# The sums of the down projection's weights in a DeepNorm decoder layer: made by transfers in DRAM from slab 6 on, in place of GpSimd beside the feed-forward slabs

## The chip, the cores and the metric

The kernel runs on one core of a Trainium2 chip. The metric is the device time of one execution, in microseconds (us), lower is better. The core has a matrix engine (PE, TensorE), a vector engine (DVE), a scalar engine (ACT), GpSimd (POOL) and an engine that only issues transfers (SP); all of them have queues of their own and meet through semaphores. 16 DMA engines carry the transfers of all queues.

## What is computed

One post-norm decoder layer on x of 512 tokens by 1024 channels, all in float32. The attention half comes first, then the channel mixer, whose last product is the one that the change is about:

```
proj   = x @ w_in                     # q,k,v of two attentions, forget logits, two gates
o_f    = forgetting_attention(...)    # 8 heads of 64
o_s    = sliding_window_sink_attention(...)
merged = sigmoid(g_f) * (o_f @ w_o_fox) + sigmoid(g_s) * (o_s @ w_o_swa)
h      = layer_norm(alpha * x + merged @ w_out)
ff     = (silu(h @ w_gate) * (h @ w_up)) @ w_down      # w_down: 2816 x 1024
out    = layer_norm(alpha * h + ff)
```

## The kernel before

Every float32 product is made of three matmuls: each operand is split into a high part, a float32r copy that ACT makes (`sh`, `xh`, `ah`), and a low part, the difference that DVE makes (`sl`, `xl`, `al`); PE adds high times high, low times high and high times low (L1375 to L1377, L1688 to L1690).

Weights come as **slabs** of 128 x 1024 elements, 512 KB each: 0 to 5 the queries, keys and values of the sliding window, 6 to 17 those of the forgetting attention, 18 to 33 the gates, 34 to 41 the output projections of the two branches, 42 to 49 w_out, 50 to 93 the gate and up matrices of the feed-forward. SP loads slab n into one of two buffers `raw` (L438) as soon as the low part of slab n - 2 has been made. ACT makes the high part of slab n (L574, L805 in the feed-forward) while PE works on slab n - 3, and DVE the low part behind it (L847, L855). ACT and DVE are in-order engines, and their programs are written out step by step: in step n ACT evicts the result of slab n - 1, takes the transposed probabilities and the exponentials of the attention units of that step, and then calls `slab_hi(n + 3)`. A unit is one head's attention: scores before a slab, its softmax on DVE and ACT, its transposes after the second of the slab's eight column blocks, and its product with the values two slabs later. Units 0 to 7 (sliding window) have their scores in steps 6 to 13, units 8 to 15 (forgetting attention) in steps 19 to 26. In steps 16 to 18 there are no units at all.

The **down projection** is made by a scheme of seven products instead of eight. For a pair of 128-row blocks of w_down (11 pairs) and its two column halves there are four quarters W11, W12, W22, W21, each 128 x 512. Besides them the scheme needs the sums

```
T1 = W11 + W12      T3 = W12 + W22      T2 = T1 + W22      T4 = T2 + W21
```

of all 11 pairs. They lie in an internal DRAM tensor `tw` of 11 x 4 x 128 x 512 floats (11.5 MB), and SP and ACT wait for all of them (semaphore `t_stored`) before the first of the 77 items of the down projection, which SP loads at L460, from `tw` or from the weights.

Before the change POOL makes the sums in the feed-forward stage: `weight_sums(i)` waits for the 1 MB load of pair i (`stage`, L523), makes the sums with three additions (L530, L533, L535), stores them (`tw`, L537) and issues the next load. Between two pairs POOL makes three sums of hidden activations (`hidden_sums`, L546 to L549), which need the results of the feed-forward slabs. Ahead of all that POOL's program holds four rotary multiplications (L500; the last one belongs to slab 5), the loads of the residual and of the first layer norm's parameters once all 16 attention units are done (`pv_done`, L503 to L505), and three halves of layer norm rows (L512). DVE reads `res` from that load for the first time at L1094.

Of the kernel before, what the change touches and what calls it, by code (L numbers as in the profile page):

```python
# [24 lines left out]
ALU = mybir.AluOpType  # L25
# [6 lines left out]
P = 128  # L32
# [18 lines left out]
N_QF = 6  # L51
# [18 lines left out]
PAIRS = FT // 2  # L70
# [3 lines left out]
W11, W12, W22, W21 = range(4)  # L74
T1, T3, T2, T4 = range(4)
# [97 lines left out]
def program(nc, xT, x, slabs, vk_slabs, wdn, rope, rope_tok, sel, b_forget, sinks, ln1_g, ln1_b, ln2_g, ln2_b, out):  # L173
    ctx = ExitStack()
    with ctx:
        base = -(-nc.sbuf_base // 64) * 64

        def at(name, kb, shape, dt=F32):
            return nc.alloc_sbuf_tensor_at(name, shape, dt, offset=base + int(kb * 1024))

        def sem(name):
            return ctx.enter_context(nc.semaphore(name))
# [3 lines left out]
        xl = at("xl", 16, [P, KC, SEQ], F32R)  # L186
        mh = at("mh", 0, [P, KC, SEQ], F32R)
        ml = at("ml", 16, [P, KC, SEQ], F32R)
        stage = at("stage", 0, [P, 4, 512])
        tsum = at("tsum", 8, [P, 4, 512])  # L190
        ah = at("ah", 0, [P, RING, 2 * P], F32R)
        al = at("al", 8, [P, RING, 2 * P], F32R)
        sg = at("sg", 16, [P, 2, SEQ])
# [69 lines left out]
        tw = nc.dram_tensor("tw", (PAIRS, 4, P, 512), F32, kind="Internal").ap()  # L263
# [26 lines left out]
        slab_done = sem("slab_done")  # L290
# [64 lines left out]
        hT_ready = sem("hT_ready")  # L355
        silu_done = sem("silu_done")
        ff_done = sem("ff_done")
        stage_landed = sem("stage_landed")
        t_summed = sem("t_summed")
        t_stored = sem("t_stored")  # L360
        part_made = sem("part_made")
        s3_made = sem("s3_made")
# [22 lines left out]
        def ready(n):  # L385
            return n + 1 if n < N_FF else n + 1 - len(LATE)
# [6 lines left out]
        def width_of(n):  # L393
            return KC // 2 * VK_W if n in N_VK else D

        def item_part(e):

            p, i = divmod(e, PAIRS)
            return parts[:, i, PRODUCTS[p][0] * 2 * P:(PRODUCTS[p][0] + 1) * 2 * P]

        def item_raw(e):
            return raw[:, e % DN_RAW * 512:(e % DN_RAW + 1) * 512]
# [6 lines left out]
        @block.sync  # L409
        def _(sp):  # L410
            def load(n):
                if n < FIRST:
                    src = vk_slabs[n - N_VK[0]]
                    sp.dma_start(first_raw[:, n, 0:width_of(n)], src).then_inc(first_landed[n], 16)
                else:
                    sp.dma_start(raw[:, (n % RAW) * D:(n % RAW + 1) * D], slabs[n - 2])\
                        .then_inc(slab_landed[n % RAW], 16)


            for c in range(KC):  # L420
                sp.dma_start(x_raw[:, c, :], xT[c]).then_inc(x_landed[c], 16)
                if c < 2:
                    sp.dma_start(first_raw[:, 0, PART[c]], slabs[0][:, PART[c]]).then_inc(part_landed[c], 16)
            for q in range(2):
                sp.dma_start(first_raw[:, 1, PART[q]], slabs[1][:, PART[q]]).then_inc(part_landed[2 + q], 16)
            sp.dma_start(cs[:, :, :], rope).then_inc(cs_landed, 16)
            for n in range(2, FIRST + RAW):
                load(n)
                if n == 2:
                    sp.dma_start(cs_tok[:, :, :, :], rope_tok).then_inc(cs_tok_landed, 16)  # L430

            def load_ring(first, end):

                with sp.Fori(0, (end - first) // RAW) as i:
                    for r in range(RAW):
                        n = first + r
                        sp.wait_ge(lo_ready, i * RAW + ready(n) - RAW)
                        sp.dma_start(raw[:, (n % RAW) * D:(n % RAW + 1) * D],  # L438
                                     slabs[bass.ds(i * RAW + (n - 2), 1)].rearrange("a p n -> (a p) n"))\
                            .then_inc(slab_landed[n % RAW], 16)  # L440

            load_ring(FIRST + RAW, N_FF - len(LATE))
            for k in range(len(LATE)):
                n = N_FF - len(LATE) + k
                sp.wait_ge(lo_ready, ready(n) - RAW)
                load(n)
                if k == 0:
                    sp.wait_ge(slab_done, N_WOUT)
                sp.dma_start(late_raw[:, k, :], slabs[LATE[k] - 2]).then_inc(late_landed[k], 16)
            load_ring(LATE[-1] + 1, SLABS)  # L450
            for e in range(ITEMS):
                p, i = divmod(e, PAIRS)
                _, summed, w, _, _ = PRODUCTS[p]
                if e == 0:
                    sp.wait_ge(t_stored, 16 * PAIRS)
                if e < DN_RAW:
                    sp.wait_ge(lo_ready, ready(N_DN - 2) + e // 2)
                else:
                    sp.wait_ge(item_ready, e - DN_RAW + 1)
                sp.dma_start(item_raw(e), (tw if summed else wdn)[i, w]).then_inc(item_landed[e % DN_RAW], 16)  # L460
            for t in range(TB):
                for q in range(2):

                    sp.wait_ge((ln_left, ln_right)[q], TB + t + 1)
                    cols = slice(512 * q, 512 * q + 512)
                    sp.dma_start(out[t * P:(t + 1) * P, cols], res[:, t, cols]).then_inc(out_landed, 16)
            sp.wait_ge(out_landed, 16 * 2 * TB)

        @block.gpsimd
        def _(pool):  # L470
# [22 lines left out]
            for k in range(len(N_QS)):  # L493
# [5 lines left out]
                    pool.wait_ge(rope_sum, k)  # L499
                pool.tensor_tensor(rope3[:, :], rope2[:, :], cs[:, 1, :], ALU.mult).then_inc(rope_sin, 1)  # L500

            pool.wait_ge(pv_done, UNITS)
            pool.dma_start(res[:, :, :], x.rearrange("(t p) d -> p t d", p=P)).then_inc(res_landed, 16)  # L503
            pool.dma_start(ln1p[:, 0, :], ln1_g.partition_broadcast(P)).then_inc(res_landed, 16)
# [14 lines left out]
            pool.dma_start(ln2p[:, 0, :], ln2_g.partition_broadcast(P)).then_inc(ln2_landed, 16)  # L519
            pool.dma_start(ln2p[:, 1, :], ln2_b.partition_broadcast(P)).then_inc(ln2_landed, 16)  # L520

            def load_stage(i):
                pool.dma_start(stage[:, :, :], wdn[i].rearrange("q p n -> p q n")).then_inc(stage_landed, 16)  # L523

            def weight_sums(i):

                pool.wait_ge(stage_landed, 16 * (i + 1))
                if i:
                    pool.wait_ge(t_stored, 16 * i)
                pool.tensor_tensor(tsum[:, T1:T3 + 1, :], stage[:, W11:W12 + 1, :], stage[:, W12:W22 + 1, :], ALU.add)\  # L530
                    .then_inc(t_summed, 1)
                pool.wait_ge(t_summed, 3 * i + 1)
                pool.tensor_tensor(tsum[:, T2, :], tsum[:, T1, :], stage[:, W22, :], ALU.add).then_inc(t_summed, 1)  # L533
                pool.wait_ge(t_summed, 3 * i + 2)
                pool.tensor_tensor(tsum[:, T4, :], tsum[:, T2, :], stage[:, W21, :], ALU.add).then_inc(t_summed, 1)  # L535
                pool.wait_ge(t_summed, 3 * i + 3)
                pool.dma_start(tw[i].rearrange("q p n -> p q n"), tsum[:, :, :]).then_inc(t_stored, 16)  # L537
                if i + 1 < PAIRS:
                    load_stage(i + 1)

            def part(i, k):
                return parts[:, i, k * 2 * P:(k + 1) * 2 * P]

            def hidden_sums(i):
                pool.wait_ge(ff_done, 2 * i + 2)
                pool.tensor_tensor(part(i, D5), part(i, A21), part(i, A22), ALU.subtract).then_inc(part_made, 1)  # L546
                pool.wait_ge(part_made, 3 * i + 1)
                pool.tensor_tensor(part(i, S6), part(i, D5), part(i, A11), ALU.subtract).then_inc(part_made, 1)
                pool.tensor_tensor(part(i, S7), part(i, A11), part(i, A21), ALU.subtract).then_inc(part_made, 1)  # L549

            load_stage(0)
            weight_sums(0)
            for i in range(PAIRS):
                if i + 1 < PAIRS:
                    weight_sums(i + 1)
                hidden_sums(i)
            pool.wait_ge(part_made, 3 * PAIRS)
            for i in range(PAIRS):
# [7 lines left out]
        def _(act):  # L566
# [163 lines left out]
            for n in range(1, N_WOUT + KC - WOUT_TAIL + 1):  # L730
# [18 lines left out]
                if N_WO <= n < N_WOUT:  # L749
                    m = n - N_WO  # L750
# [15 lines left out]
                if N_WO < n <= N_WOUT:  # L766
                    m = n - 1 - N_WO
# [25 lines left out]
            with act.Fori(1, FT // 2 - 1) as i:  # L793
                for r in range(4):

                    m = N_FF + r + AHEAD + 1
# [10 lines left out]
            def item_split(e):  # L807

                p, i = divmod(e, PAIRS)
                if e == 0:  # L810
                    act.wait_ge(t_stored, 16 * PAIRS)
                if p == M5:
                    act.wait_ge(part_made, 3 * i + 1)
                if e == M1 * PAIRS:
                    act.wait_ge(part_made, 3 * PAIRS)
                if p == M3:
                    act.wait_ge(s3_made, i + 1)
                if e < RING:
                    act.wait_ge(slab_done, N_DN - SPL + 1 + e // 2)
                else:  # L820
                    act.wait_ge(item_done, e - RING + 1)
                act.activation(ah[:, e % RING, :], item_part(e), ACT.Copy)
                act.wait_ge(item_landed[e % DN_RAW], 16 * (e // DN_RAW + 1))
                act.activation(item_slot(sh, e), item_raw(e), ACT.Copy).then_inc(item_hi, 1)  # L824
# [965 lines left out]
```

## Time and profile before

| | us |
|---|---|
| median of 3 runs | 705.5 (705.21 to 706.83) |
| the profiled execution, its own time | 705.27 |
| its span, from the first to the last instruction of the program | 703.5 |
| PE busy | 689.3, 98% of the span |
| DVE / ACT / POOL busy | 433.1 / 336.1 / 140.2 |
| moved by DMA | 102.09 MB, mean 145 GB/s |

The 1.8 us between the span and the time of the same execution are start and end outside the program's instructions. A busy time is the sum of an engine's instructions in the trace; PE's matmuls overlap each other, so a matmul of 512 columns is shown with 389 ns and the next starts about 230 ns after it. An engine's waits are told apart by what released it.

### The profile page before, as it was taken

Reading aid. Unit: us, or ns where it says so; the run is one execution under the profiler, and the core shown is the slowest. Engines: PE = TensorE matmul, PEld = TensorE weight load, DVE = VectorE, ACT = ScalarE, POOL = GpSimd, SP = SyncE. Lnnn points to the kernel's source line nnn. Section 1 sums busy time; section 2 is a strip of 40 time slices with the busy share of each in tenths; the row PEclk is TensorE's granted clock in tenths of the full one; section 3 lists DMA queues with packets and bytes.
Section 4 is the critical chain, followed back from the end, with each engine's and each line's share of the span. In section 5 each row is a group of like instructions: output and inputs, shape, how many; then the busy total and the mean of one; then the engine's idle time right before and its main releaser. Section 6 shows DMA issues by size and latency. Waiting matters only on the chain.

```text
span 703.5 us, 9442 instructions
## 1 busy us (share of the span) xinstructions
PE 689.3 (98%) x3380; PEld 577.5 (82%) x3380; DVE 433.1 (62%) x739; ACT 336.1 (48%) x624; POOL 140.2 (20%) x129
## 2 busy tenths in 40 slices
PE   8999999999999999999999999999999999999985
PEld 6987888888888888888998888888888888888863
DVE  5669997767876236647923433333334337988997
ACT  6678787467766344433222222222222225677741
POOL 2110000000001000000245565355533415100000
PEclk9999999999999999999999999999999999999998
DMA  8221112211113522351357666654466433676643
GB/s 322 76 91 61 61 67 84 90 60 61 61 61 133 225 90 91 115 214 61 105 186 247 210 223 224 209 195 157 163 230 209 150 110 99 187 218 209 186 129 135
DMA packets 34723, 102.09 MB, mean 145 GB/s; under 512 B 3584, under 2 KB 3712, under 8 KB 34688
## 3 DMA queue, kind: packets, MB, share of 16 engines
q1 hardware_dynamic: 27504, 74.36, 31.1%
q0 software_dynamic: 7184, 27.27, 11.6%
q8 instruction: 20, 0.33, 0.2%
q14 instruction: 15, 0.12, 0.1%
HBM read 87.99 MB, written 13.63 MB: 144 GB/s over the span
## 4 chain that ended last, share of the span: by engine, by line
PE 77%; DVE 10%; DMA 6%; ACT 4%; issue 2%; POOL 0%; SPq 0%; DVEq 0%; ACTq 0%
PE ps L1375 23%; PE ps L1377 23%; PE ps L1376 23%; DVE sl L855 4%; DMA raw<-tw 3%; DMA raw<-in_wdn 2%; PE ps L1457 2%; DVE al L855 2%; PE ps L1443 2%; PE ps L1413 1%; ACT rope L590 1%; PE ps L1408 1%; ACT sh L824 1%; DMA x_raw<-in_xT 1%; PE ps L1418 1%
## 5 line engine op out<-in xcount | busy, mean ns | idle before, releaser
L855 DVE TENSOR_TENSOR sl<-raw,sh 128x512 fp32r<-128x512 f32 (+1 forms) x113 | 113.6, 1006 | 76.6 <-ACT sh L805 76.6
L1375 PE MATMUL ps<-hTh,sh 128*128 128x512 f32 x320 | 124.5, 389 | 0.0
L1376 PE MATMUL ps<-hTh,sl 128*128 128x512 f32 x320 | 124.5, 389 | 0.0
L1377 PE MATMUL ps<-hTl,sh 128*128 128x512 f32 x320 | 124.5, 389 | 0.0
L805 ACT ACTIVATE sh<-raw 128x1024 fp32r<-128x1024 f32 x36 | 38.2, 1062 | 146.5 <-PE ps L1377 137.3
L847 DVE TENSOR_TENSOR sl<-raw,sh 128x1024 fp32r<-128x1024 f32 x50 | 61.8, 1235 | 54.5 <-ACT sh L574 54.3
L1375 PE MATMUL ps<-xh,sh 128*128 128x512 f32 x224 | 90.4, 404 | 1.0 <-DVE xl L1181 0.8
L1377 PE MATMUL ps<-xl,sh 128*128 128x512 f32 x224 | 87.6, 391 | 0.0
L1376 PE MATMUL ps<-xh,sl 128*128 128x512 f32 x224 | 87.3, 390 | 0.0
L574 ACT ACTIVATE sh<-raw 128x1024 fp32r<-128x1024 f32 x50 | 52.9, 1059 | 43.0 <-PE ps L1377 36.4
L1376 PEld LDWEIGHTS ps<-hTh,sl 128*128 128x128 f32 x320 | 60.1, 188 | 12.5
L1375 PEld LDWEIGHTS ps<-hTh,sh 128*128 128x128 f32 x320 | 60.1, 188 | 12.5
L1377 PEld LDWEIGHTS ps<-hTl,sh 128*128 128x128 f32 x320 | 60.1, 188 | 12.3
L1688 PE MATMUL ps<-sh,ah 128*128 128x512 f32 x154 | 60.6, 393 | 2.9 <-DVE res L1296 2.1
L824 ACT ACTIVATE sh<-raw 128x512 fp32r<-128x512 f32 x77 | 48.2, 626 | 28.3 <-DMA raw<-in_wdn 14.3
L1690 PE MATMUL ps<-sl,ah 128*128 128x512 f32 x154 | 59.9, 389 | 0.0
L1689 PE MATMUL ps<-sh,al 128*128 128x512 f32 x154 | 59.9, 389 | 0.0
L1375 PEld LDWEIGHTS ps<-xh,sh 128*128 128x128 f32 x224 | 42.1, 188 | 10.0 <-DVE xl L1181 2.3
L1377 PEld LDWEIGHTS ps<-xl,sh 128*128 128x128 f32 x224 | 42.0, 188 | 9.2
L1376 PEld LDWEIGHTS ps<-xh,sl 128*128 128x128 f32 x224 | 42.2, 188 | 7.4
L855 DVE TENSOR_TENSOR al<-parts,ah 128x256 fp32r<-128x256 f32 x77 | 35.9, 466 | 16.2 <-ACT sh L824 15.9
L1275 DVE TENSOR_TENSOR parts<-sg,ps 128x512 f32 x18 | 12.4, 688 | 46.9 <-PE ps L1377 46.9
(211 smaller groups left out, 1268.2 us busy)
## 6 DMA issues: line engine op xcount, KB each, us to landing
raw<-in_slabs SPq DMA_DIRECT2D x86, 512.0 KB, 3.3
stage<-in_wdn POOLq DMA_DIRECT2D x11, 1024.0 KB, 9.0
tw<-tsum POOLq DMA_DIRECT2D x11, 1024.0 KB, 5.7
raw<-tw SPq DMA_DIRECT2D x44, 256.0 KB, 2.8
raw<-in_wdn SPq DMA_DIRECT2D x33, 256.0 KB, 2.8
x_raw<-in_xT SPq DMA_DIRECT2D x8, 256.0 KB, 5.1
res<-in_x POOLq DMA_DIRECT2D x1, 2048.0 KB, 9.7
late_raw<-in_slabs SPq DMA_DIRECT2D x4, 512.0 KB, 4.3
```

Source lines behind the costliest of these rows:

```text
L574: act.activation(slot(sh, n, width_of(n)), raw_of(n), ACT.Copy).then_inc(hi_ready, 1)
L805: act.activation(slot(sh, m), raw_of(m), ACT.Copy).then_inc(hi_ready, 1)
L824: act.activation(item_slot(sh, e), item_raw(e), ACT.Copy).then_inc(item_hi, 1)
L847: dve.tensor_tensor(slot(sl, n, w), raw_of(n), slot(sh, n, w).bitcast(F32), ALU.subtract).then_inc(lo_ready, 1)
L855: return dve.tensor_tensor(dst, src, hi.bitcast(F32), ALU.subtract)
L1375: pe.matmul(dst, lh, rh, start=start, stop=False)
L1376: pe.matmul(dst, ll, rh, start=False, stop=False)
L1377: return pe.matmul(dst, lh, rl, start=False, stop=stop)
L1443: last = pe.transpose(ps[:, 5 + col // 512, col % 512:col % 512 + P], prob[:, off + (kb - k0) * P:off + (kb - k0 + 1) * P], ident[:, :])
L1688: pe.matmul(dst, lh, rh, start=start, stop=False, skip_group_check=True)
L1689: pe.matmul(dst, ll, rh, start=False, stop=False, skip_group_check=True)
L1690: last = pe.matmul(dst, lh, rl, start=False, stop=stop, skip_group_check=True)
```

## The change

`stage` and `tsum` and the semaphores `stage_landed` and `t_summed` are gone, and so are POOL's load, three additions and store for each pair. In their place POOL issues eight transfers between the last rotary multiplication and the wait for `pv_done`. Each takes one quarter of all 11 pairs at once (2.88 MB). Four are copies from DRAM to DRAM (`first_term`), and four add (`add_term`): the DMA engines read the quarter of `tw` and the quarter of the weights, and write the sum back to `tw`. A transfer that reads what another one wrote waits for its semaphore on POOL. `t_stored` now comes to 32, from the last transfers of T3 and T4.

```diff
@@ SP, and likewise ACT's item_split
                 if e == 0:
-                    sp.wait_ge(t_stored, 16 * PAIRS)
+                    sp.wait_ge(t_stored, 32)
@@ POOL, behind the last rotary multiplication
+            def whole(source, k):
+                return source[:, k, :, :].rearrange("i (a b) n -> i a (b n)", b=4)
+
+            def first_term(k, source, m, done):
+                pool.dma_start(whole(tw, k), whole(source, m)).then_inc(done, 16)
+
+            def add_term(k, m, done):
+                pool.dma_start(whole(tw, k), whole(wdn, m), accum_op=ALU.add, max_dma_last_dim=8192).then_inc(done, 16)
+
+            pool.wait_ge(slab_done, N_QF)
+            first_term(T1, wdn, W11, t_part)
+            first_term(T3, wdn, W12, t_part)
+            pool.wait_ge(t_part, 32)
+            add_term(T1, W12, t_part)
+            add_term(T3, W22, t_stored)
+            pool.wait_ge(t_part, 48)
+            first_term(T2, tw, T1, t_part)
+            pool.wait_ge(t_part, 64)
+            add_term(T2, W22, t_part)
+            pool.wait_ge(t_part, 80)
+            first_term(T4, tw, T2, t_part)
+            pool.wait_ge(t_part, 96)
+            add_term(T4, W21, t_stored)
+
             pool.wait_ge(pv_done, UNITS)
@@ POOL, in the feed-forward stage
-            def load_stage(i):
-                pool.dma_start(stage[:, :, :], wdn[i].rearrange("q p n -> p q n")).then_inc(stage_landed, 16)
-
-            def weight_sums(i):
-
-                pool.wait_ge(stage_landed, 16 * (i + 1))
-                if i:
-                    pool.wait_ge(t_stored, 16 * i)
-                pool.tensor_tensor(tsum[:, T1:T3 + 1, :], stage[:, W11:W12 + 1, :], stage[:, W12:W22 + 1, :], ALU.add)\
-                    .then_inc(t_summed, 1)
-                pool.wait_ge(t_summed, 3 * i + 1)
-                pool.tensor_tensor(tsum[:, T2, :], tsum[:, T1, :], stage[:, W22, :], ALU.add).then_inc(t_summed, 1)
-                pool.wait_ge(t_summed, 3 * i + 2)
-                pool.tensor_tensor(tsum[:, T4, :], tsum[:, T2, :], stage[:, W21, :], ALU.add).then_inc(t_summed, 1)
-                pool.wait_ge(t_summed, 3 * i + 3)
-                pool.dma_start(tw[i].rearrange("q p n -> p q n"), tsum[:, :, :]).then_inc(t_stored, 16)
-                if i + 1 < PAIRS:
-                    load_stage(i + 1)
@@
-            load_stage(0)
-            weight_sums(0)
             for i in range(PAIRS):
-                if i + 1 < PAIRS:
-                    weight_sums(i + 1)
                 hidden_sums(i)
```

PE, DVE, ACT and SP keep their instructions in the same order. On POOL, this is the program from the rotary multiplications to the second pair of sums before the change (the names: `tw` the sums in DRAM, `in_wdn` the weights of the down projection, `parts` the hidden activations):

```order
L500 TENSOR_TENSOR rope_67<-rope_66,cs 128x512 x4
L503 DMA res<-in_x 128x4x1024
L504 DMA ln1p<-in_ln_g 128x1024
L505 DMA ln1p<-in_ln_b 128x1024
L512 TENSOR_TENSOR res<-res,ln1p 128x512 x3
L519 DMA ln2p<-in_ln_g 128x1024
L520 DMA ln2p<-in_ln_b 128x1024
L523 DMA stage<-in_wdn 128x4x512
L530 TENSOR_TENSOR tsum<-stage 128x1024
L533 TENSOR_TENSOR tsum<-tsum,stage 128x512
L535 TENSOR_TENSOR tsum<-tsum,stage 128x512
L537 DMA tw<-tsum 128x4x512
```

and this is the same place with the change (line numbers of the changed kernel):

```order
L497 TENSOR_TENSOR rope_65<-rope_64,cs 128x512 x4
L505 DMA tw<-in_wdn 11x4x16384 x2
L508 DMA tw<-in_wdn 11x32x2048 x2
L505 DMA tw<-tw 11x4x16384
L508 DMA tw<-in_wdn 11x32x2048
L505 DMA tw<-tw 11x4x16384
L508 DMA tw<-in_wdn 11x32x2048
L526 DMA res<-in_x 128x4x1024
L527 DMA ln1p<-in_ln_g 128x1024
L528 DMA ln1p<-in_ln_b 128x1024
L535 TENSOR_TENSOR res<-res,ln1p 128x512 x3
```

What moved: all work on `tw` stands ahead of the load of `res`, and the load of `res` now comes behind the wait for the last copy. A copy is made of rows of 16384 elements (64 KB) each, an adding transfer of rows of 2048 elements (8 KB).

## Rows read from the trace of the kernel before

**Rows 1.** The page: span, and busy time of each engine.

```profile
span 703.5 us, 9442 instructions
PE 689.3 (98%) x3380; PEld 577.5 (82%) x3380; DVE 433.1 (62%) x739; ACT 336.1 (48%) x624; POOL 140.2 (20%) x129
```

**Rows 2.** The longest waits of PE and the one in the attention: waiter, releaser, us in total, times, longest.

```profile
PE ps L1688 <- DVE res L1296: 2.1, 1, 2.1
PE ps L1566 <- POOL stack L475: 1.7, 1, 1.7
...
PE ps L1408 <- ACT prob L651: 0.7, 1, 0.7
```

**Rows 3.** Busy time by stage: us, then busy (instructions) of PE to POOL, clock, DMA.

```profile
45.00:112.00 67.00, 66.26 (x377) 55.75 (x376) 60.60 (x143) 54.46 (x136) 1.29 (x1) 1.00 0.18 64
...
340.00:560.00 220.00, 220.00 (x1071) 186.46 (x1070) 86.07 (x84) 55.58 (x67) 108.49 (x85) 1.00 0.58 200
```

**Rows 4.** The last store of the sums (POOL, L537), and SP's first item load.

```profile
553.29 0.78 POOL L537 DMA_DIRECT2D tw<-tsum  x1 [0.30 <-POOL tsum L535]
DMA to landing us min/median/max: 5.3/5.3/5.3
...
561.77 11.85 SPq L460 DMA_DIRECT2D raw<-tw  x6
```

**Rows 5.** POOL in order of time: the last rotary multiplication, then the loads for the residual.

```profile
51.21 1.29 POOL L500 TENSOR_TENSOR rope<-rope,cs 128x512 f32<-128x512 f32 x1 [7.33 <-ACT rope L590]
...
222.91 0.81 POOL L503 DMA_DIRECT2D res<-in_x  x1 [170.40 <-PE ps L1457]
223.71 0.55 POOL L504 DMA_DIRECT2D ln1p<-in_ln_g  x1
224.24 0.53 POOL L505 DMA_DIRECT2D ln1p<-in_ln_b  x1
```

**Rows 6.** DVE's first use of the residual: times, first and last start.

```profile
L1094 DVE SCALAR_TENSOR_TENSOR res<-res,ps x8: 674/680/689, 325.5 to 345.5; 128x512 f32<-128x512 f32 x8
```

**Rows 7.** DMA rate beside those loads: columns as in rows 3, last GB/s.

```profile
227.00:229.00 2.00, 2.00 (x10) 1.65 (x10) 0.00 (x0) 0.83 (x2) 0.00 (x0) 1.00 1.02 412
```

**Rows 8.** DMA issues of the page: KB each, median us to landing.

```profile
raw<-in_slabs SPq DMA_DIRECT2D x86, 512.0 KB, 3.3
...
res<-in_x POOLq DMA_DIRECT2D x1, 2048.0 KB, 9.7
...
ln1p<-in_ln_g POOLq DMA_DIRECT2D x1, 512.0 KB, 11.2
ln1p<-in_ln_b POOLq DMA_DIRECT2D x1, 512.0 KB, 13.1
```

**Rows 9.** The slab load issued among them, and the instruction that waited for it.

```profile
L438 SPq DMA_DIRECT2D raw<-in_slabs x1: 333/333/333, 227.1 to 227.1; - x1
DMA to landing us min/median/max: 7.7/7.7/7.7
...
234.87 1.06 ACT L574 ACTIVATE sh<-raw 128x1024 fp32r<-128x1024 f32 x1 [0.67 <-DMA raw<-in_slabs]
```

**Rows 10.** The slab load of 53.8 us, and ACT's use of it.

```profile
L438 SPq DMA_DIRECT2D raw<-in_slabs x1: 333/333/333, 53.8 to 53.8; - x1
...
66.50 1.04 ACT L574 ACTIVATE sh<-raw 128x1024 fp32r<-128x1024 f32 x1
```

**Rows 11.** A softmax's last step on DVE, and the transposes that need it.

```profile
68.85 1.07 DVE L1027 TENSOR_SCALAR prob<-prob,rden 128x128 f32<-128x128 f32 x4
...
70.55 0.93 PE L1443 MATMUL ps<-ident,prob 128*128 128x128 f32 x7
```

**Rows 12.** A slab load in the stretch without units, and ACT there.

```profile
L438 SPq DMA_DIRECT2D raw<-in_slabs x1: 333/333/333, 126.9 to 126.9; - x1
...
130.46 1.06 ACT L574 ACTIVATE sh<-raw 128x1024 fp32r<-128x1024 f32 x1 [4.08 <-PE ps L1377]
...
136.31 2.07 ACT L632 ACTIVATE v_f<-ps 128x512 fp32r<-128x512 f32 x4 [4.79 <-PE ps L1377]
```

More of the change, by code:

```diff
@@ L188, in program @@
         ml = at("ml", 16, [P, KC, SEQ], F32R)
-        stage = at("stage", 0, [P, 4, 512])
-        tsum = at("tsum", 8, [P, 4, 512])
         ah = at("ah", 0, [P, RING, 2 * P], F32R)
@@ L357, in program @@
         ff_done = sem("ff_done")
-        stage_landed = sem("stage_landed")
-        t_summed = sem("t_summed")
+        t_part = sem("t_part")
         t_stored = sem("t_stored")
@@ L810, in item_split @@
                 if e == 0:
-                    act.wait_ge(t_stored, 16 * PAIRS)
+                    act.wait_ge(t_stored, 32)
                 if p == M5:
```

## The prediction

> **What bounds the kernel now.** I read the page's busy times first, then PE's waits, then the busy time by stage. PE is busy for 689.3 of 703.5 us [rows 1], and no wait of PE is over 2.1 us; the only one in the attention half is 0.7 us [rows 2]. In the feed-forward stage, where POOL now makes the sums, PE is busy 220 of 220 us, although POOL works 108 us there and the DMA engines 58% of the time [rows 3]. So what the change takes away in that stage hides under a full PE. In the attention stage PE is busy 66.3 of 67 us, but there DVE (60.6) and ACT (54.5) are nearly full as well, and the DMA engines are idle for four fifths of it [rows 3]. It is into this stage that the change puts its transfers. The question is then only whether the slab loads, which share the 16 DMA engines with them, still land in time.
>
> **What is removed.** Eleven loads of 1 MB, 33 additions and 11 stores leave a stage in which PE never waits: worth 0 us. Where the sums are waited for, nothing is won either: the last store starts at 553.3 and lands 5.3 us later, at 558.6, while SP's first item load starts at 561.8 [rows 4]; SP waited there for a low part, not for the sums. Cost of the removal 0, gain 0. The slab loads of the feed-forward land sooner, which PE does not notice.
>
> **What is added: the chain of transfers.** POOL can start when its last rotary multiplication is over, 51.2 + 1.3 = 52.5 us [rows 5]; the wait for slab 5 is over by then. Each pass covers 11 x 128 x 512 x 4 bytes = 2.88 MB. No transfer between two DRAM tensors stands in this trace. The nearest row is the load of the residual, at 412 GB/s, with the engines full [rows 7]: 2.88 MB would take 7.0 us. That is the lower end for a copy. The upper end is twice that, 14 us, if a byte read from and a byte written to DRAM both count. I take 10, nearer the middle since both ends are equally far. An adding pass reads two bytes and writes one for each byte: 14 to 28 us by the same reckoning, I take 20. A dependent pass follows 2 us later (a slab load of 1.3 us at that rate lands after 3.3 [rows 8], so 2 us are fixed). The order is then: copies of T1 and T3, 2 + 20, until 75; both additions, 2 + 40, until 117; copy T2, 12, until 129; addition, 22, until 151; copy T4, 12, until 163; addition, 22, until about 185 us. With both ends of each pass it would be 145 to 230 us.
>
> What waits behind this on POOL is the load of the residual, issued at 222.9 now [rows 5] and needed at 325.5 [rows 6]; it lands 9.7 us after issue and its last companion after 13.1 [rows 8], so the chain may last until about 311 before anybody notices. I cost this at 0. The feed-forward's hidden sums on POOL no longer alternate with weight sums: 0.
>
> **What a slab load suffers.** A load issued by itself lands after 3.3 us [rows 8]. One was issued at 227.1, when POOL had 3 MB under way, and landed after 7.7, at 234.8 [rows 9]. The residual, issued at 222.9, landed at 232.6, and the layer norm rows issued at 223.7 at 234.9 [rows 5, 8]. So a slab load does not overtake much: it landed behind the 2 MB issued before it and about together with the next transfer. I apply that to the passes.
>
> The room is this. The load issued at 53.8 is used by ACT at 66.5 [rows 10], that is 12.7 us later. ACT takes the slab without a choice of order, and behind it stand the evictions and exponentials of the next unit. DVE ends a softmax at 68.85 + 1.07 = 69.9 and PE turns its result at 70.55 [rows 11]: 0.6 us of room. With DVE 90% full there (60.6 of 67), a slab load that lands later than 12.7 us after its issue costs PE nearly all of the excess.
>
> - **First pair of copies.** The load of 53.8 is issued 1.3 us behind them. It lands when they are nearly through: 52.5 + 2 + 20 + 1.3 = 75.8 instead of 66.5 at the latest. ACT stands for 9.3 us; less 0.6 of room and about 1 that ACT can catch up, PE loses **8 us**. Ends: 0 if the load gets its turn after 7.7 us; with a pair at 28 us it is 17 less 1.6 = 15.
> - **Adding passes, 80 us in all.** Beside a plain stream a load loses 7.7 - 3.3 = 4.4 us. If each of the neighbours' bytes costs two or three times as much, it is 8.8 or 13.2, and the load lands after 12.1 to 16.5 us. I take 14 us. Two loads are in flight, so the excess over 12.7 costs each slab half: 0.65 us, for some 8 slabs, **5 us**. Ends: 0, and 1.9 x 8 = 15.
> - **The stretch without units.** There slabs follow each other within 5.5 us, and the load issued at 126.9 is used at 130.5, only 3.6 us later, but the next task that PE needs of ACT is the eviction of the values at 136.3 [rows 12]. A load that lands after 14 us comes at 140.9, so ACT is 4.6 us late, and with its own instruction of 1.06 some 5: I take **4 us**. Ends 0 and 7.
> - **Copies of T2 and T4.** A load issued at their start lands after 3.3 + 10 = 13.3: 0.6 over the room each, **1 us**. Ends 0 and 4.
>
> Sum: 8 + 5 + 4 + 1 = 18 us. The profiled execution took 705.27 us, 0.2 under the median of 705.5, so I forecast 705.3 + 18 = **723 us**. The ends add up to +0 and +41.
>
> The Trainium skill, "DMA: Bandwidth & Descriptors", section "Why a DMA increments its semaphore by 16 and not by 1", says that a transfer is split over the largest number of engines, at most 16, that divides the slowest dimension on both sides. The slowest dimension of the eight transfers is 11, so by that rule each would run on 11 of the 16 engines, and a pass would take 16/11 as long: 10 us for the copy at the rate of the residual's load, which is what I took, and 14 to 20 at the upper end, by which the first term would reach its own upper end. No row before shows a transfer of this kind.
>
> **The rivals.**
>
> *Fair shares, no loss.* The engines take packets of the two queues in turn, so a slab load loses only its share: 7.7 us as in rows 9, at most 12.1 beside the adding passes. All of that is inside the 12.7 us of room, and only the stretch without units could lose a fraction. Time 705 to 706.5, say 705.5, not slower. For it: the load of rows 9 did land before the last transfer issued ahead of it (224.2 + 13.1 = 237.4 [rows 8]), and ACT waited only 0.7 us. Against: it came behind the residual's 2 MB, and a row of 64 KB, one sixteenth of a megabyte in one piece, leaves few places to take turns. It decides if the latencies stay under 12.7 us. The Trainium skill names this rule in the same page, section "Queues, rings and completion order": each engine goes round its queues, changing only at packet boundaries. By it this rival would be the likely one.
>
> *Only the small part.* Copies are cut up and do not block, adding passes do a little: 5 + 4, or the first pair alone, 8. Time 709 to 714.
>
> *Strict order of arrival.* A slab load waits for all that POOL has issued before it. Then the first pair costs up to 15, the pair of additions 40 - 12.7 = 27, the two single additions 20 - 12.7 = 7 each, the copies 1: 57 us, 762. For it: the residual's load was let through first. Against: the mixture with the layer norm rows.
>
> *The chain is slow.* If an adding pass takes over 55 us instead of 20, the chain ends after 311 and the residual comes late: every microsecond beyond that is a microsecond of PE, on top of the losses above, so over 765.
>
> *Faster.* It would need a stall in the feed-forward stage or at the first item that the change lifts, and the rows show none. Only scatter is left.
>
> **How the numbers follow.** About 0.2% (1.4 us) is what a measurement can tell. Chances: forecast 0.48; small part 0.14; strict order or slow chain 0.14; fair shares 0.20; faster 0.04. Slower by over 0.2%: 0.48 + 0.14 + 0.14 = 0.76. Within: 0.20. Faster: 0.04. The likeliest time is 723. The range begins at 705, to take in fair shares, and ends at 750, which covers the forecast's upper end but for a little; the strict order and half of the faster outcomes lie outside. The forecast's own range is 714 to 745.
>
> **What the changed profile would show.** Right: on POOL eight issues between 52.5 us and about 185; ACT's splits of slabs with waits for `raw` of several us, the first near 66; PE waits for ACT or DVE between 66 and 185 that add up to some 18 us, where rows 2 have 0.7; DMA full in those slices; the feed-forward as before, 220 of 220. Wrong: slab loads landing under 12.7 us throughout and PE as full as before (fair shares); waits of PE for the residual at 325 us and later (slow chain); any gain or loss behind slab 50, which I have cost at nothing.

## The result, and the profile after

The changed kernel takes 729.05 us (median of 4 runs, 723.79 to 731.43) where the kernel before takes 705.5: 1.032 times as long, with a 95% interval of 1.030 to 1.034. Its profiled execution has a span of 727.6 us, 24.1 more than the 703.5 of [rows 1]. The four executions lie 7.6 us apart; the account below is that of the profiled one alone. Its page gives the engines, the fill of 40 slices of 18.2 us each, the clock of PE in tenths, and what the copies in DRAM did to the totals:

```profile
span 727.6 us, 9385 instructions
PE 696.7 (96%) x3380; PEld 583.6 (80%) x3380; DVE 423.9 (58%) x739; ACT 337.2 (46%) x624; POOL 68.2 (9%) x82
...
PE   8999499979999999999999999999999999999985
...
PEclk9999699999999999999999999999999999999998
DMA  8138698377641453235013232332232232577643
...
HBM read 99.53 MB, written 25.17 MB: 171 GB/s over the span
```

The same two rows on the page of before:

```profile
PE   8999999999999999999999999999999999999985
...
PEclk9999999999999999999999999999999999999998
```

The new holes in PE's row lie in the fifth and the ninth slice, 73 to 91 us and 146 to 164 us, in the attention half. PE's waits (waiter, releaser, us in total, times, longest) name three that are new, the first three of these:

```profile
PE ps L1408 <- ACT prob L651: 10.7, 2, 9.9
PE ps L1408 <- DVE q_aug L995: 3.7, 1, 3.7
PE ps L1475 <- DVE stack L978: 3.6, 1, 3.6
PE ps L1688 <- DVE res L1296: 2.1, 1, 2.1
PE ps L1566 <- POOL stack L472: 1.7, 1, 1.7
```

The two of 10.7 together hold the 0.7 of [rows 2], so 17.3 us are new. None of the releasers is a transfer: in the first stall PE waits for a softmax, and the softmax waits for ACT, which stands in front of a slab. The load that [rows 10] showed issued at 53.8 us, and ACT and PE behind it:

```profile
L435 SPq DMA_DIRECT2D raw<-in_slabs x1: 333/333/333, 54.1 to 54.1; - x1
...
DMA to landing us min/median/max: 25.9/25.9/25.9
```

```profile
79.95 1.06 ACT L574 ACTIVATE sh<-raw 128x1024 fp32r<-128x1024 f32 x1 [13.04 <-DMA raw<-in_slabs]
...
85.83 1.22 PE L1408 MATMUL ps<-kh_s,q_s 128*128 128x128 f32 x4 [9.93 <-ACT prob L651]
```

It landed 25.9 us after its issue, ACT stood for 13.0 us, and PE's scores of the next unit started 9.9 us late. POOL's issues show what was under way (start, duration of the issue, idle time before it and what ended it):

```profile
52.77 1.19 POOL L505 DMA_DIRECT2D tw<-in_wdn  x2
80.03 2.29 POOL L508 DMA_DIRECT2D tw<-in_wdn  x2 [26.06 <-DMA tw<-in_wdn]
108.07 0.58 POOL L505 DMA_DIRECT2D tw<-tw  x1 [25.76 <-DMA tw<-in_wdn]
143.69 1.09 POOL L508 DMA_DIRECT2D tw<-in_wdn  x1 [35.04 <-DMA tw<-tw]
171.54 0.58 POOL L505 DMA_DIRECT2D tw<-tw  x1 [26.76 <-DMA tw<-in_wdn]
184.67 1.15 POOL L508 DMA_DIRECT2D tw<-in_wdn  x1 [12.55 <-DMA tw<-tw]
246.88 0.82 POOL L526 DMA_DIRECT2D res<-in_x  x1 [61.06 <-PE ps L1457]
```

The slab load landed at 54.1 + 25.9 = 80.0 us, and ACT used it at once; the pair of copies was through at 52.8 + 1.2 + 26.1 = 80.0 us, the same moment. What the DMA engines did in between can be read from the trace's packets. From 60 to 67 us (queue of POOL's transfers, then queue of the slab loads: packets, MB, share of 16 engines):

```profile
q0 software_dynamic: 33, 2.10, 90.2%
q1 hardware_dynamic: 36, 0.15, 6.1%
```

2.10 MB in 32 rows of 64 KB (the 33rd packet is a small one), beside 36 rows of 4 KB of slab loads: one row of each in turn, and not one queue before the other. A row of 64 KB takes some 7 x 16 x 0.902 / 32 = 3.2 us of an engine. A slab load has 128 rows, 8 for each of 16 engines; eight turns of 3 us are 24 to 26 us, about what it took.

The copy of T2, issued at 108 beside the still running addition of T3, took 35.3 us; the slab load issued at 127.0 landed 16.6 us later, and PE stood 3.6 us. That stall went over DVE: the low part of the late slab stands ahead of the forget gates' rows (`stack`) that PE needed (start, us, instruction, idle time before it):

```profile
144.72 1.23 DVE L847 TENSOR_TENSOR sl<-raw,sh 128x1024 fp32r<-128x1024 f32 x1 [5.39 <-ACT sh L574]
```

Beside the addition of T2 a load issued at 146.1 landed after 12.2 us, and PE stood 3.7 us. The loads for the residual come at 246.9 instead of 222.9, delayed by PE's own lateness (`pv_done`), not by the chain, which POOL had issued whole by 186 us.

The waits are 17.3 of 24.1 us. The rest is the clock. Before, it was at its full level throughout the attention. Now (columns as in [rows 3]: stretch, busy PE, PEld, DVE, ACT, POOL, granted clock, DMA share, GB/s):

```profile
75.00:85.80 10.80, 0.90 (x4) 0.39 (x3) 4.65 (x9) 5.60 (x15) 2.29 (x2) 0.66 0.46 109
85.80:92.00 6.20, 6.17 (x24) 5.32 (x25) 5.97 (x17) 3.35 (x5) 0.00 (x0) 0.50 1.02 227
92.00:112.00 20.00, 20.00 (x118) 16.99 (x117) 17.24 (x39) 15.33 (x38) 0.58 (x1) 1.00 1.01 244
146.00:151.00 5.00, 3.59 (x13) 2.93 (x14) 4.11 (x12) 0.00 (x0) 0.00 (x0) 0.66 0.75 167
163.00:168.00 5.00, 4.11 (x16) 3.45 (x17) 2.39 (x6) 2.69 (x4) 0.00 (x0) 0.66 0.79 199
355.00:580.00 225.00, 225.00 (x1102) 190.73 (x1101) 84.57 (x103) 57.50 (x72) 32.22 (x32) 1.00 0.27 91
```

After the stall PE works 6.2 us at 0.50, the lower of its two levels (1.2 GHz), and does 3.1 us of work in it. After the two short stalls the mean of five microseconds is 0.66: with one level at half, that is 68% of 5 us, 3.4 us at half in each, of which it was working some 2.7 and 3.4: another 3.0 us. Waits 17.3 and clock 3.1 + 3.0 make 23.4 of the 24.1 us. PE's busy time bears this out roughly: it is 7.4 us longer than before (696.7 against 689.3) for the same 3380 matmuls. The last row is the feed-forward: PE 225 of 225, as in [rows 3], with POOL down from 108 to 32 us and DMA from 58% to 27%. Nothing was gained there.

### The profile page after: what moved, and what is told of

It reads as the page before. It is cut to its first block, busy times and chain, and to the rows that moved or that the text cites. A ratio compares the mean times of both kernels' runs of the same rounds, so it can differ in the third digit from the quotient of the medians.

```text
span 727.6 us, 9385 instructions
## 1 busy us (share of the span) xinstructions
PE 696.7 (96%) x3380; PEld 583.6 (80%) x3380; DVE 423.9 (58%) x739; ACT 337.2 (46%) x624; POOL 68.2 (9%) x82
## 4 chain that ended last, share of the span: by engine, by line
PE 66%; DMA 15%; DVE 12%; ACT 4%; issue 2%; POOL 0%; SPq 0%; DVEq 0%; ACTq 0%
PE ps L1375 20%; PE ps L1377 20%; PE ps L1376 20%; DMA raw<-in_slabs 10%; DVE sl L855 4%; DMA raw<-in_wdn 3%; DVE al L855 2%; DMA raw<-tw 2%; PE ps L1457 2%; DVE sl L847 1%; PE ps L1443 1%; ACT rope L590 1%; ACT sh L824 1%; PE ps L1408 1%; PE ps L1413 1%
## 5 line engine op out<-in xcount | busy, mean ns | idle before, releaser
L855 DVE TENSOR_TENSOR sl<-raw,sh 128x512 fp32r<-128x512 f32 (+1 forms) x113 | 104.1, 921 | 77.8 <-ACT sh L805 77.8
L847 DVE TENSOR_TENSOR sl<-raw,sh 128x1024 fp32r<-128x1024 f32 x50 | 61.3, 1226 | 75.2 <-ACT sh L574 75.1
```

Source lines behind the costliest of these rows:

```text
L847: dve.tensor_tensor(slot(sl, n, w), raw_of(n), slot(sh, n, w).bitcast(F32), ALU.subtract).then_inc(lo_ready, 1)
L855: return dve.tensor_tensor(dst, src, hi.bitcast(F32), ALU.subtract)
```

## The experiments

The theory at this point was **A**: the change wins nothing, and each lost microsecond comes from a slab load that cannot get past rows of the new transfers; rows of 64 KB (A1) and passes piled on shared engines (A2) make it worse. The rivals were that GpSimd's work had cost something (B), that only the amount of traffic counts (C), and that the place is to blame (D).

**Without any sums.** Chain and waits are left out.

```diff
-            pool.wait_ge(slab_done, N_QF)
-            first_term(T1, wdn, W11, t_part)
...
-            add_term(T4, W21, t_stored)
@@ SP
-                if e == 0:
-                    sp.wait_ge(t_stored, 32)
...
-                sp.dma_start(item_raw(e), (tw if summed else wdn)[i, w]).then_inc(item_landed[e % DN_RAW], 16)
+                sp.dma_start(item_raw(e), wdn[i, w]).then_inc(item_landed[e % DN_RAW], 16)
```

> No sums of weights are made at all, by nobody: the down projection reads plain quarters of the weights where it should read sums, so its values are not the reference's. Theory A (what the change removes was hidden under a full PE, and all 24 us come from the added transfers in the attention stage): 704.5 to 706 us, the same as before, PE waits as in the kernel before. Rival B (the sums on GpSimd did cost something in the feed-forward stage, which the changed kernel has given back): 700 us or less, and the added transfers then cost more than the 24 us seen.

Measured: 705.59 us, 1.000 times before (0.999 to 1.001). With neither GpSimd's sums nor the transfers the time is that of before. B is out: what the change removes was worth nothing, and the loss is all in the added chain.

**Copies in rows of 8 KB.**

```diff
             def first_term(k, source, m, done):
-                pool.dma_start(whole(tw, k), whole(source, m)).then_inc(done, 16)
+                pool.dma_start(whole(tw, k), whole(source, m), max_dma_last_dim=8192).then_inc(done, 16)
```

> As the changed kernel, but the four copies are cut into rows of 8 KB instead of 64 KB; still 11 engines. Theory A1 (a slab load cannot get between rows of 64 KB, and that gives the stall of 10.3 us beside the first pair of copies and the one of 3.6 beside the copy of T2): the load issued at 54 lands after under 12 us, the first stall is below 2 us, its half clock is gone, and the time falls by 10 to 17 us, to 712 to 718. Rival C (only the amount of traffic on the engines counts, whatever its rows): the same stalls, 726 to 731.

Measured: 712.26 us, 1.009 (1.007 to 1.011). The pair of copies is no faster; the additions can be issued at 81.95 us instead of 80.03. But the slab load of 54 us is let through in 9.6 us instead of 25.9, inside its 12.7 us of room, and PE does not stall there at all:

```profile
52.45 1.43 POOL L505 DMA_DIRECT2D tw<-in_wdn  x2
81.95 2.27 POOL L508 DMA_DIRECT2D tw<-in_wdn  x2 [28.07 <-DMA tw<-in_wdn]
```

```profile
L435 SPq DMA_DIRECT2D raw<-in_slabs x1: 333/333/333, 53.8 to 53.8; - x1
...
DMA to landing us min/median/max: 9.6/9.6/9.6
```

That is 16.8 of the 23.5 us, for the same bytes over the same time: C is out, A1 stands. One stall is left:

```profile
PE ps L1375 <- DVE bias_l L988: 4.1, 1, 4.1
```

**Sixteen engines.** The row numbering is turned round, on top of the copies in rows of 8 KB.

```diff
             def whole(source, k):
-                return source[:, k, :, :].rearrange("i (a b) n -> i a (b n)", b=4)
+                return source[:, k, :, :].rearrange("i (a b) n -> a i (b n)", b=4)
```

> As e2, and with the rows numbered so that the slowest dimension is 32 instead of 11: the same bytes over 16 engines. Theory A2 (11 is what confines each pass to 11 engines, and two passes pile up on six of them): passes take some 11/16 of the time of e2, the adding pass 12.6 + 2 = 20 us or less for 22 rows of 8 KB at 0.63 us per engine, the chain ends 40 us earlier; time 708 to 714, a few us under e2. Rival C: total work on the engines is the same, so a slab load suffers the same: within 2 us of e2.

Measured: 709.34 us, 1.006 (1.004 to 1.008). Both copies are through at 75.1 us instead of 82.0, the addition of T1 takes 19 us instead of 28, and the last addition is issued at 152 instead of 188 us. So with 32 as the slowest dimension the additions are a quarter to a third shorter. A copy by itself hardly is: from its issue to the next, that of T4 takes 12.7 us here and 14.2 with 11 as the slowest dimension. (The sum in the expectation is off: 22 rows at 0.63 us and 2 us are 16, not 20; 19 were measured.) A slab load beside a pass is no better off, 10.3 us for that of 54 against 9.6. One stall of 2.5 us is left, and it lies in the stretch without units, where the one load that ACT needs soon after its issue ([rows 12]: 3.6 us) lands after 10.8 to 11.7:

```profile
L435 SPq DMA_DIRECT2D raw<-in_slabs x2: 333/333/333, 126.8 to 129.5; - x2
...
DMA to landing us min/median/max: 10.8/11.2/11.7
```

```profile
138.53 1.06 ACT L574 ACTIVATE sh<-raw 128x1024 fp32r<-128x1024 f32 x1 [12.18 <-DMA raw<-in_slabs]
```

**The same chain beside the feed-forward.** `whole`, `first_term` and `add_term` as in the changed kernel.

```diff
-            pool.wait_ge(slab_done, N_QF)
-            first_term(T1, wdn, W11, t_part)
...
@@ behind the loads of ln2p
+            first_term(T1, wdn, W11, t_part)
...
+            add_term(T4, W21, t_stored)
```

> The eight transfers exactly as in the changed kernel, but issued behind the first layer norm, beside the feed-forward slabs. Theory D (it is the place: in the attention ACT and DVE have no room, in the feed-forward they idle and PE has two slabs in stock, about 10 us): loads land as late as before, up to 26 us after issue, ACT waits as long, but PE loses only what is beyond 5 + 10 us, one stall of 5 to 10 us at the first pair of copies and small ones after: 712 to 722. Rival C (place is nothing): 726 to 731. If PE has more stock than I think: 706.

Measured: 736.49 us, 1.043 (1.042 to 1.045), worse than in the attention, and outside what I expected. PE has room for one late slab, not for a row of them. In 400 to 440 us it is busy 28.3 of 40 us, and in the feed-forward it waits nine times for DVE's products (`parts`), 20.8 us in all, where before no wait of PE is listed in that stage:

```profile
PE ps L1375 <- DVE parts L1275: 20.8, 9, 5.9
...
400.00:440.00 40.00, 28.34 (x116) 22.05 (x114) 6.39 (x7) 6.58 (x8) 1.68 (x2) 0.96 0.64 189
```

ACT waited for slab loads 17 times, 116.6 us in all. The second line is that of the 20 loads issued while the chain ran (362 to 507 us):

```profile
ACT sh L805 <- DMA raw<-in_slabs: 116.6, 17, 12.3
...
DMA to landing us min/median/max: 4.8/11.4/17.5
```

There a slab is used up every 5.44 us (24 matmuls), with two loads in flight, and the loads took 11.4 us in the median, up to 17.5. So D as I put it is wrong: the feed-forward is not the roomier place for this form of the chain.

**Only the first pair.** The other six transfers are left out, in the attention, rows of 64 KB; the products that would need them read plain quarters of the weights, so the kernel leaves out part of the sums.

```diff
             first_term(T1, wdn, W11, t_part)
             first_term(T3, wdn, W12, t_part)
-            pool.wait_ge(t_part, 32)
...
-            add_term(T4, W21, t_stored)
```

> Of the eight transfers only the first two are left, the copies of T1 and T3 in rows of 64 KB at their old moment; the additions and T2 and T4 are left out, and the items that would read them read plain quarters, so the values of the down projection are not the reference's. Theory A1 (this pair alone gives the stall of 10.3 us and the 14 us of half clock after it, a good 3 us lost): the load issued at 54 lands after 26 us, one stall of 10 us, 718 to 719. Rival (the stall needs the later passes behind it, or most of the 24 us are from the adding passes): under 714.

Measured: 719.09 us, 1.019 (1.017 to 1.020): 13.4 us over before. The load landed after 26.3 us, PE's stall is 10.3, and 2.6 us go to the clock, which is 0.58 in the mean over the 6.3 us of work behind the stall. (The 14 us at half that the expectation names begin in the stall itself; only the part in which PE works costs anything.) More than half of the change's loss is this one load beside this one pair.

```profile
85.72 1.00 PE L1397 MATMUL ps<-kh_s,q_s 128*128 128x128 f32 x3 [10.33 <-ACT prob L640]
```

**The copies apart.**

```diff
             first_term(T1, wdn, W11, t_part)
+            pool.wait_ge(t_part, 16)
             first_term(T3, wdn, W12, t_part)
```

> As the changed kernel, rows of 64 KB and 11 engines, but the copy of T3 is issued only when that of T1 has landed. Theory A2 (both copies pile up on the engines that they share, and the slab load of 54 us must wait for both): it lands after 13 to 16 us instead of 26, the first stall is 0 to 3 us instead of 10, and the time 714 to 719, although the chain is some 3 us longer. Rival F (any pass in rows of 64 KB blocks the loads as long as it runs, and two in a row block twice): the load of 54 waits 13 us and the next again; two stalls, 726 to 731.

Measured: 717.71 us, 1.017 (1.015 to 1.019). The copies take 13.5 and 14.5 us one after the other, hardly more together than the pair's 27.3. The load of 54 lands after 12.7 us, just inside its room, the next one after 6.5, and the first stall is gone. So the late load is not repeated at each pass: F is out. With the copies apart a load meets the rows of one of them and not of both. Whether two copies are bad by their number of rows alone or because they share engines (A2), this run does not tell apart; rows of 64 KB on sixteen engines were not run. Two stalls stay, from the passes of T2, as in the changed kernel (3.8 and 2.8 us):

```profile
PE ps L1376 <- DVE bias_l L989: 3.8, 1, 3.8
PE ps L1409 <- DVE q_aug L996: 2.8, 1, 2.8
```

**Sixteen engines, and no pass in the stretch without units.** On top of the kernel on sixteen engines, with all rows of 8 KB:

```diff
             pool.wait_ge(t_part, 48)
+            pool.wait_ge(slab_done, N_G + 1)
             first_term(T2, tw, T1, t_part)
```

> As e3 (rows of 8 KB, 16 engines), but the copy of T2 and all behind it wait until slab 18 is done, so that no pass runs in the stretch without units. Theory E (what e3 still loses, a stall of 2.8 us at 141, comes from T2's addition in that stretch, where a slab load is used 3.6 us after its issue): no wait of PE over 1 us in the attention, 705 to 706.5. Rival (the rest is spread over many loads): 708 to 710 as e3.

Measured: 705.77 us, 1.000 (0.999 to 1.001). The pass of T2 starts at 142.7 us, loads in the attention still land after up to 11.7 us, and PE has no wait over 0.8 us there. The whole rest of the loss on sixteen engines was that one stretch.

**Rows of 4 KB.** Sixteen engines as above, with no pause in the chain.

```diff
-                return source[:, k, :, :].rearrange("i (a b) n -> a i (b n)", b=4)
+                return source[:, k, :, :].rearrange("i (a b) n -> a i (b n)", b=2)
```

> As e3, but all eight transfers in rows of 4 KB, the size of a slab load's own rows. Theory A3 (the engines take one row of each queue in turn, so a slab load beside an adding pass pays one row of it for each of its own 8): the loads beside the adding passes land after 3.3 + 8 x 0.3 = 6 to 8 us instead of 10, and the stall in the stretch without units is gone or under 1 us: 705.5 to 707.5. Rival G (what counts is how far a queue's rows are fetched ahead in bytes or in number, or the cost of a short addition does not shrink): as e3, 708 to 711, or slower if a row of 4 KB costs as much as one of 8 KB and the chain gets longer.

Measured: 705.70 us, 1.000 (0.999 to 1.001). The time is as expected, the latencies only in part: beside the first pair the load still takes 9.1 us, and the four issued from 118 to 137 us take 8.5 in the median and 9.2 at most, where the two above took 10.8 and 11.7. ACT's wait there falls from 12.2 to 2.0 us, and PE's is gone. I had expected 6 to 8 us beside an addition; a row of half the size does not halve the wait. Part of the gain in the stretch is a matter of moments: the load that ACT needs 3.6 us after its issue, at 126.7 us here, fell between the copy of T2 and its addition (issued at 127.7) and landed after 3.3 us. The next experiment covers what this one leaves open.

**Rows of 4 KB on eleven engines.** `max_dma_last_dim` is 4096 for copies and additions, so that rows are not joined again.

```diff
-                return source[:, k, :, :].rearrange("i (a b) n -> a i (b n)", b=2)
+                return source[:, k, :, :].rearrange("i (a b) n -> i a (b n)", b=2)
```

> Rows of 4 KB as in e8, but with 11 as the slowest dimension again, so 11 engines. Theory A3 (the row's size alone decides what a slab load pays per row of its own; the number of engines sets only how long the chain is and how many loads it meets): loads beside the passes land after 8 to 10 us as in e8, no stall beside the attention, at most 2 us in the stretch without units, 705.5 to 708. Rival A2 (the engines that two passes share are what hurts, whatever the rows): 710 to 713 as e2.

Measured: 705.84 us, 1.000 (0.999 to 1.001). The chain is as long as in the changed kernel (last addition issued at 192 us), and nothing is lost. Here the load that ACT needs soon, issued at 127.4 us, does meet the copy of T2 and takes 8.0 us, and PE still has no wait over 0.7 us in the attention. With rows of 4 KB the eleven engines cost nothing. What they add where rows are large is not shown: with rows of 8 KB the kernel on sixteen engines was 2.9 us faster, but its chain is also shorter and meets other loads.

**Rows of 4 KB beside the feed-forward.** Sixteen engines, at the place where the chain in rows of 64 KB did worst.

```diff
-                return source[:, k, :, :].rearrange("i (a b) n -> i a (b n)", b=4)
+                return source[:, k, :, :].rearrange("i (a b) n -> a i (b n)", b=2)
...
-            pool.wait_ge(slab_done, N_QF)
-            first_term(T1, wdn, W11, t_part)
...
@@ behind the loads of ln2p
+            first_term(T1, wdn, W11, t_part)
...
```

> The form of e8 (rows of 4 KB, 16 engines) at the place of e4, beside the feed-forward slabs. Theory H (there a slab is used up every 5.44 us and two loads are in flight, so a load may take at most about 2 x 5.44 - 2.3 of splitting = 8.6 us in the long run; what is beyond costs half of it per slab, and PE's stock is spent after a few): loads land after 8 to 10 us, PE loses up to 0.7 us per slab for some 20 slabs after its stock is gone: 706 to 714. Rival D (the feed-forward has more room than the attention, and e4 failed only by its rows of 64 KB): 705.5.

Measured: 705.42 us, 1.000 (0.999 to 1.001). H expected a loss and D none; D's number is the right one here. ACT waits for slabs 18 times, 75.5 us in all, the 23 loads issued while the chain ran (362 to 479 us) take up to 11.5 us, and PE is still busy 40 of 40:

```profile
ACT sh L805 <- DMA raw<-in_slabs: 75.5, 18, 9.2
...
DMA to landing us min/median/max: 3.2/8.0/11.5
```

```profile
400.00:440.00 40.00, 40.00 (x178) 33.10 (x178) 12.35 (x13) 10.43 (x12) 1.30 (x1) 1.00 1.00 283
```

The median of 8.0 us is a little under the 8.6 that by the expectation's estimate two loads in flight can bear in the long run (2 x 5.44 - 2.3), and single ones of 11.5 go out of PE's stock. In the changed form of the transfers the median was 11.4, over that bound. The two kernels differ in row size and in number of engines together, so how much each of them gives in this place was not tried. None of the ten is faster than before; with PE full wherever the chain can be hidden, they show nothing that could be.

## Why the prediction was right

The forecast was 723 us with a range of 705 to 750; measured are 729.

- **The removal is worth 0:** right, shown by the kernel without sums and by PE's 225 of 225.
- **First pair of copies, 8 us:** the path is right, step by step: the load was expected to land at 75.8, it landed at 80.0, because the pair took 27 us and not 22. ACT stood 13.0 instead of 9.3, PE 9.9 instead of 8. The reason given, that a load hardly overtakes what was issued before it, is not what the trace shows. The engines do take turns, row by row, and the load ends with the pair because each of its few rows waits for a row of 64 KB; that the two end together is in part luck. Alone this pair cost 13.4 us, and most of what is not the stall is a term that the sum did not have: **the half clock after the stall**, 3.1 us in the changed kernel.
- **Adding passes beside units, 5 us:** too much. The five loads issued from 82 to 118 us landed after 10.8 to 15.5 us, 12.7 in the median, where I had taken 14; of the slowest ACT waited for 1.0 us, and PE has no wait between 92 and 143 us. With a median of 12.7, just the room, there was hardly an excess, so the price of half of it for each slab was not put to the test; the latency was what was too high. (That of the transfers was too low: an addition took 26 to 28 us, where I had 20.)
- **The stretch without units, 4 us:** right in kind, too small. It gave one stall of 3.6 and one of 3.7 instead of one of 4, each with its own half clock. The second is the one reckoned, over the eviction of the values; the first went over DVE and the forget gates, which I had not looked at. The chain ran 28 us longer than reckoned (last transfer landing at 213 us instead of 185): 5 us at the first pair, 9 in the two additions and the copy of T2, which ran beside that of T3 and took 35.3 us, 1 at the copy of T4, and 6 and 7 at the last two additions. So this stretch met a copy in rows of 64 KB, which I had placed earlier, and an addition behind it. How much this stretch matters is shown by the kernel whose passes keep out of it: there the loss went from 3.6 us to nothing.
- **Copies of T2 and T4, 1 us:** the copy of T4 did nothing; that of T2 is in the point before.
- **The chain does not delay the residual, 0:** right.

The waits measured are 17.3 us, against 18 forecast; that agreement is in part luck, since the terms of the first pair and of the stretch were too small (8 and 4, against 9.9 and 7.3) and those of the additions and later copies too large (5 and 1, against nothing).

Of the rivals, fair shares was right that the engines take turns and wrong that this makes the loss small: with rows of 64 KB a turn is some 3 us. With rows of 4 KB its time came out too. Strict order is refuted by the additions, beside which it had a load wait for up to 40 us and where the loads took 10.8 to 15.5. The Trainium skill, "DMA: Bandwidth & Descriptors", section "Queues, rings and completion order", lets an engine change queues at the end of a packet. The trace agrees: 32 rows of 64 KB and 36 of 4 KB start in the same 7 us, and one row of 64 KB is one packet. The load of 54 us takes 25.9, 9.6 and 7.7 us beside the same bytes in rows of 64, 8 and 4 KB, all with 11 as the slowest dimension, and 10.3 and 9.1 us in rows of 8 and 4 KB with 32 and 64. Why the small rows still cost 4 to 7 us over the 3.3 of a load alone stays open. The rule on the number of engines, in the section "Why a DMA increments its semaphore by 16 and not by 1", agrees in part. In rows of 8 KB the addition of T1 takes 28.4 us with a slowest dimension of 11 and 19.3 with one of 32, a ratio of 1.47 where 16/11 is 1.45; but for the addition of T2 the ratio is 1.31 (26.0 and 19.8), and for the copy of T4 1.11 (14.2 and 12.7). The trace does not say which engine moved a packet.

## What to carry to other kernels

Before a transfer is moved to a stage with idle DMA engines, read there how long after its issue each load is used, the shortest, not the mean: here some 10 to 17 us in most of the attention, but 6.5 and 3.6 us for the loads issued at 118.8 and 126.9. A background transfer is safer in rows as small as those of the loads it shares the engines with: with rows of 4 KB the same 23 MB of sums cost nothing in either place, with rows of 8 KB they cost nothing only where no pass met that stretch. And a stall on a PE that is otherwise full has to be priced with the half clock that can follow it: here the stalls of 3.6 us and more had it, the one of 2.5 us had not.

## What the runs showed of the hardware that was not expected

- A pair of copies from DRAM to DRAM in rows of 64 KB held a 512 KB load back for as long as it ran: 25.9 us instead of 3.3. The engines took rows of the two queues one for one (32 and 36 in 7 us), and a row of 64 KB took some 3 us. Cut into rows of 8 KB the pair took 29.5 us itself, against 27.3, so the large rows gave it little.
- An addition in DRAM of 2.88 MB in rows of 8 KB took 26 to 28 us beside slab loads with 11 as the slowest dimension and 19 to 20 with 32; a copy of the same size and rows took 14.2 and 12.7 us, and 13.5 in rows of 64 KB.
- A stall of 3.6 us in an otherwise full PE already brought 3.4 us at the lower clock level, from just before its end, of which PE worked 2.7; one of 10 us brought a drop during the stall itself and 6.2 us of work at half. The stall of 2.5 us of the kernel on sixteen engines left no mark; its clock from 138 to 150 us is 1.00.
